# Halving the columns of the score levels, feeding output tiles by k-tile, dividing the query product and adding unread products in a two-block fp32 kernel

## The reference

```python
# block 1: one mixer of two halves, then a pool mixer, a conv FFN behind each
z = h @ w_in                                   # q, f, i, g of HGRN; q, k, v of window attention
diff = b[:, :, :, None, :] - b[:, :, None, :, :]          # b = cumsum(log f) in a chunk
att = einsum('bhtk,bhsk,bhtsk->bhts', qb, kb, exp(where(causal, diff, -inf)))
o = o_inter + att @ vb                         # 4 heads of 128; S carried from chunk to chunk
y = concat([oa, ob]) @ w_out                   # out1
# block 2, layer 0: Fourier mixing and a gated linear attention in both directions
o_f = gla_scan(q, k, v, loga[0]); o_b = gla_scan(flip(q), flip(k), flip(v), flip(loga[1]))
y = concat([fourier_mix(u_f), norm(o_f + flip(o_b)) * silu(r)]) @ w_out       # out2
# block 2, layer 1: grouped attention, 8 query heads on 2 key heads, 512 queries, 768 keys
q = rope(rms_norm(h @ w_q)); p = softmax(q @ k.T / sqrt(128)); y = (p @ v) @ w_att_out  # attout
# layer norms (block 1) and rms norms (block 2) stand between all stages
```

## Time and profile before

| | |
|---|---|
| median of three executions | 3099.12 us (3098.80 to 3101.23) |
| profiled execution | 3098.91 us |
| its span, first to last instruction | 3097.3 us |
| busy PE / weight loads / DVE / ACT / POOL | 2644.9 (85%) / 2172.8 (70%) / 1810.3 (58%) / 1082.0 (35%) / 21.5 (1%) |
| mean granted TensorE clock | 0.916 |
| DMA | 295.50 MB, mean 95 GB/s |

### The profile page before, as it was taken

One profiled execution on the slowest core, in us unless ns is written; L12 is line 12 of the kernel. 1 busy time (PEld: TensorE's weight loads), 2 busy tenths in 40 slices (PEclk: granted clock), 3 DMA queues, 4 the chain that ended last, 5 costly groups with the idle time before them and its releaser, 6 DMA issues.

```text
span 3097.3 us, 31671 instructions
## 1 busy us (share of the span) xinstructions
PE 2644.9 (85%) x12904; PEld 2172.8 (70%) x12904; DVE 1810.3 (58%) x2446; ACT 1082.0 (35%) x1419; POOL 21.5 (1%) x31
## 2 busy tenths in 40 slices
PE   5945579999659999898655889999998977889998
PEld 4844458888438888687355678888887765768886
DVE  6575568888778877610386255524543556465464
ACT  2242253233353244422222243312332544353242
POOL 0000000000010000000000000000000000000000
PEclk9977789999879999999765799999999998999999
DMA  8700027855115666221000012211121100123232
GB/s 309 237 20 2 31 78 265 275 188 183 47 63 184 198 203 199 67 99 40 18 1 1 21 48 68 68 64 57 66 68 63 41 21 14 54 77 109 87 101 83
DMA packets 80272, 295.50 MB, mean 95 GB/s; under 512 B 8944, under 2 KB 11632, under 8 KB 79872
## 3 DMA queue, kind: packets, MB, share of 16 engines
q1 hardware_dynamic: 80128, 293.49, 28.4%
HBM read 291.35 MB, written 2.10 MB: 95 GB/s over the span
## 4 chain that ended last, share of the span: by engine, by line
PE 77%; DVE 14%; ACT 6%; issue 2%; DMA 0%; POOL 0%; DVEq 0%; ACTq 0%
PE ps L308 65%; PE ps L331 2%; PE ps L2114 1%; PE ps L1668 1%; DVE gatt L672 1%; PE ps L661 1%; DVE p_lo L2384 1%; DVE anm L2366 1%; DVE h_lo L513 1%; DVE w_lo L288 1%; DVE hatt L672 1%; DVE x L1244 0%; DVE x L1257 0%; ACT h_hi L507 0%; PE ps L916 0%
## 5 line engine op out<-in xcount | busy, mean ns | idle before, releaser
L308 PE MATMUL ps<-h_hi,w_hi 128*128 128x512 f32 (+1 forms) x2448 | 821.1, 371 | 90.1 <-DVE w_lo L288 39.2
L308 PE MATMUL ps<-h_lo,w_hi 128*128 128x512 f32 (+1 forms) x2448 | 816.1, 369 | 0.0
L308 PE MATMUL ps<-h_hi,w_lo 128*128 128x512 f32 (+1 forms) x2448 | 815.0, 369 | 0.0
L288 DVE TENSOR_TENSOR w_lo<-w_raw,w_hi 128x1024 fp32r<-128x1024 f32 (+2 forms) x323 | 414.7, 1284 | 573.4 <-ACT w_hi L280 572.5
L280 ACT ACTIVATE w_hi<-w_raw 128x1024 fp32r<-128x1024 f32 (+2 forms) x323 | 357.2, 1106 | 892.9 <-PE ps L308 871.9
L308 PEld LDWEIGHTS ps<-h_hi,w_hi 128*128 128x128 f32 x2448 | 464.3, 190 | 178.7 <-issue 54.8
L308 PEld LDWEIGHTS ps<-h_lo,w_hi 128*128 128x128 f32 x2448 | 464.6, 190 | 78.8 <-issue 1.0
L308 PEld LDWEIGHTS ps<-h_hi,w_lo 128*128 128x128 f32 x2448 | 464.2, 190 | 79.0
L308 PE MATMUL ps<-g_hi,w_hi 128*128 128x512 f32 (+1 forms) x880 | 295.9, 369 | 0.8 <-DVE w_lo L288 0.8
L308 PE MATMUL ps<-g_lo,w_hi 128*128 128x512 f32 (+1 forms) x880 | 294.9, 368 | 0.0
L308 PE MATMUL ps<-g_hi,w_lo 128*128 128x512 f32 (+1 forms) x880 | 294.9, 368 | 0.0
(11 more groups left out here) (370 smaller groups left out, 2724.7 us busy)
## 6 DMA issues: line engine op xcount, KB each, us to landing
w_raw<-in_up SPq DMA_DIRECT2D x176, 512.0 KB, 3.3
m_raw<-in_w_mod SPq DMA_DIRECT2D x96, 512.0 KB, 3.3
w_raw<-in_down SPq DMA_DIRECT2D x64, 704.0 KB, 4.1
m_raw<-in_ada_w SPq DMA_DIRECT2D x83, 512.0 KB, 4.7
w_raw<-in_in SPq DMA_DIRECT2D x39, 512.0 KB, 3.3
w_raw<-in_out SPq DMA_DIRECT2D x16, 512.0 KB, 3.3
m_start<-in_ada_w SPq DMA_DIRECT2D x13, 512.0 KB, 12.0
w_raw<-in_qkv SPq DMA_DIRECT2D x12, 512.0 KB, 3.2
```

The source lines that it names most:

```text
L288: dve.tensor_tensor(k.w_lo[s][:, 0:w], k.w_raw[s][:, 0:w], k.w_hi[s][:, 0:w].bitcast(F32), ALU.subtract).then_inc(*k.tick("w_lo", g))
L308: last = pe.matmul(ps[:, bank, 0:tn], a[:, c, :], b[:, c, t0:t0 + tn], start=c == 0 and n == 0, stop=c == kt - 1 and n == 2)
```

## The change

Four parts.

1. **Half-column levels.** Step 0 and levels 0 and 1 stay whole. From level 2 on PE multiplies only the receiving half of each unit's columns (64, taken with strides from the same operand), the results lie side by side, and DVE's copy takes half as many columns. Such a step has two groups (HGRN 8 and 8 units, GLA 8 and 16) and its banks alternate by the step's parity: 4 to 7 and 0 to 3. The masks are 1664 columns (HGRN) and 5760 (GLA) where they were 1024 and 1920; SP loads 704 and 1280. POOL makes them with one cast per step, repeating them, 8 and 15 casts where there was one each.
2. **Output tiles.** out1: ACT splits tile 1 ahead of the vectors. out2: tiles 0 and 1 as a pair, each k-tile as soon as it is there; tile 1's split goes into GLA's loop of the heads. attout: tiles 0 and 1 in parts inside the last period and around mix 7, and tile 1's split ahead of mix 7's copy.
3. **Divided query product.** Chunks 0 to 2 at t=0, 3 and 4 at t=1, 5 to 7 at t=3, each part ahead of the score; in bank 3, the sum, rotation and mixes in bank 1, mix 7 in bank 0. ACT's copy of the product stands at t=3, what follows it (sum, root, norm, rotation, q_hi, q_lo) a period later, at t=0, 1 and 3. Head 0 to 5's h_hi and h_lo move from periods 7 to 9 to periods 8 and 9.
4. **Fillers.** pe_sums puts 8 products of ones by ones (128 columns, float32) ahead of its wait and 14 behind the sums; nobody reads them.

```diff
+def is_wide(steps, i):
+    return i == 0 or steps[i - 1][1] < WIDE
+def halves(a, step):
+    backward, level = step
+    half = 1 << level
+    return a.rearrange("p (n c) -> p n c", c=2 * half)[:, :, 0 if backward else half:half if backward else 2 * half]
...
+def pool_masks(k, label, masks, att, directions):
+    pool, src, at = k.nc.gpsimd, mask_stage(att, directions), 0
+    steps = (HG_STEPS, GL_STEPS)[directions - 1]
+    for i in range(len(steps) + 1):
+        n = mask_width(steps, i)
+        part = src[:, at:at + n]
+        last = pool.tensor_copy(mask_of(masks, steps, i).rearrange("p (u c) -> p u c", c=n), part.unsqueeze(1).to_broadcast([P, 1 if n == P else 4 * directions, n]))
+        at += n
+    last.then_inc(*k.tick("masks", label))
...
+def score_groups(steps, i, n_units):
+    if is_wide(steps, i):
+        return [(0, 4, 4), (8, 12, 4)] if n_units == 16 else [(0, 4, 4), (8, 16, 4), (12, 20, 4)]
+    return [(0, 4, 4), (8, 12, 4)] if n_units == 16 else [(0, 4, 4), (8, 16, 8)]
+def score_bank(steps, i, g):
+    return 4 + 2 * (g % 2) if is_wide(steps, i) else (4 if i % 2 else 0) + 2 * g
+def pe_scores(k, label, i, lhs, rhs, units, steps):
+    pe, wide, groups = k.nc.tensor, is_wide(steps, i), score_groups(steps, i, len(units))
+    before = max([j for j in range(i) if (wide or i % 2 if is_wide(steps, j) else j % 2 == (1 if wide else i % 2))], default=None)
+    for g, (first, second, n) in enumerate(groups):
+        if wide and g >= 2:
+            pe.wait_ge(*k.seen("att", (label, i, g - 2)))
+        elif before is not None and is_wide(steps, before) and wide:
+            pe.wait_ge(*k.seen("att", (label, before, g if g + 2 >= len(groups) else g + 2)))
+        elif before is not None:
+            pe.wait_ge(*k.seen("att", (label, before, len(score_groups(steps, before, len(units))) - 1 if wide or is_wide(steps, before) else g)))
+        bank = score_bank(steps, i, g)
+        for u in range(n):
+            for side, at in enumerate((first, second)):
+                rows, cols = units[at + u]
+                width = mask_width(steps, i)
+                out, right = k.ps[:, bank + side, u * width:(u + 1) * width], rhs[rows, cols]
+                if not wide:
+                    out, right = out.rearrange("p (n c) -> p n c", c=1 << steps[i - 1][1]), halves(right, steps[i - 1])
+                last = pe.matmul(out, lhs[rows, cols], right, start=True, stop=True)
+        last.then_inc(*k.tick("scored", (label, i, g)))
+def dve_scores(k, label, i, att, masks, n_units, steps):
+    dve, mask = k.nc.vector, mask_of(masks, steps, i)
+    if i:
+        dve.wait_ge(*k.seen("att", (label, i - 1, len(score_groups(steps, i - 1, n_units)) - 1)))
+    for g, (first, second, n) in enumerate(score_groups(steps, i, n_units)):
+        dve.wait_ge(*k.seen("scored", (label, i, g)))
+        bank = score_bank(steps, i, g)
+        got = k.ps[:, bank:bank + 2, :]
+        dst = att[:, first:second + n, :].rearrange("p u c -> p (u c)")
+        if second - first > n:
+            dst = att[:, 8:24, :].rearrange("p (s u) c -> p s u c", s=2)[:, :, first - 8:first - 8 + n, :].rearrange("p s u c -> p s (u c)")
+        else:
+            dst = dst.rearrange("p (s c) -> p s c", s=2)
+        if is_wide(steps, i):
+            dst, got = (a.rearrange("p s (u c) -> p s u c", c=P) for a in (dst, got))
+            chosen = mask.unsqueeze(1).unsqueeze(1).to_broadcast([P, 2, 4, P])
+        else:
+            backward, level = steps[i - 1]
+            half = 1 << level
+            dst = dst.rearrange("p s (n c) -> p s n c", c=2 * half)[:, :, :, 0 if backward else half:half if backward else 2 * half]
+            got = got[:, :, 0:n * P // 2].rearrange("p s (n c) -> p s n c", c=half)
+            chosen = mask[:, 0:n * P // 2].rearrange("p (n c) -> p n c", c=half).unsqueeze(1).to_broadcast([P, 2, n * P // 2 // half, half])
+        dve.copy_predicated(dst, chosen, got).then_inc(*k.tick("att", (label, i, g)))
...
+def pe_filler(k, n):
+    for _ in range(n):
+        k.nc.tensor.matmul(k.ps[:, 4, 0:P], k.ones[:, :], k.ones[:, :], start=True, stop=True)
...
+    pe_filler(k, 8)
...
+    pe_filler(k, 14)
...
+        if h == 3:
+            act_split(k, BASE["out2"] + 1)
...
+    ready = [("h_lo", ("fourier", c)) for c in range(4)] + [("h_lo", ("gla", c)) for c in range(4, KD)]
+    pe_residual(k, BASE["out2"], TALL, k.h_hi, k.h_lo, ready, ("rms", 1), paired=True)
...
+PARTS = [range(0, 3), range(3, 5), range(0), range(5, 8)]
+QUERY_BANK, SUM_BANK = 3, 1
...
     for p in range(2, PERIODS):
-        if p < HEADS:
-            pe_query(k, p, [("roped", ("q", p - 1 if p > 2 else 0, "sin"))])
-        if p == 2:
-            pe_query_turn(k, 1)
         for t, s in enumerate(steps_of(p)):
+            if p < HEADS:
+                pe_query(k, p, PARTS[t])
+            if p == PERIODS - 1:
+                pe_attout_part(k, 0, (range(2), range(2, 3), range(3, 4), range(4, 5))[t])
             pe_score(k, s)
             if t == 2 and p >= 3:
                 pe_mix(k, p - 3)
             if s >= 2:
                 pe_probs(k, s - 2)
-            if t == 1 and p < HEADS:
-                pe_query_sum(k, p)
-            if t == 2 and p < HEADS:
-                pe_query_turn(k, p)
-    for s in (4 * HEADS - 2, 4 * HEADS - 1):
-        pe_probs(k, s)
+            if t == 0 and p <= HEADS:
+                pe_query_sum(k, p - 1)
+            if t == 1 and p <= HEADS:
+                pe_query_turn(k, p - 1)
+    pe_probs(k, 4 * HEADS - 2)
+    pe_attout_part(k, 0, range(5, 6))
+    pe_probs(k, 4 * HEADS - 1)
+    pe_attout_part(k, 1, range(2))
     pe_mix(k, HEADS - 1)
-def pe_query(k, p, free):
-    pe_product(k, QKV + 4 + p, LAT, k.h_hi, k.h_lo, (), at_bank(p), free)
+    pe_attout_part(k, 1, range(2, 6))
+    for c in (6, 7):
+        for n in range(2):
+            pe_attout_part(k, n, range(c, c + 1))
...
+def mix_bank(h):
+    return SUM_BANK if h < HEADS - 1 else 0
...
+            if t == 0 and p == 2:
+                act_query(k, 1)
+            if t == 0 and p < HEADS:
+                act_split(k, QKV + 4 + p + 1)
+            if t == 3 and p < HEADS:
+                act_query(k, p)
+            if t == 1 and p <= HEADS:
+                act_query_root(k, p - 1)
             act_at_exp(k, s)
             if t == 2 and p >= 3:
                 act_mixed(k, p - 3)
             if s >= 2:
                 act_probs(k, s - 2)
-            if t == 1 and p < HEADS:
-                act_query_root(k, p)
-            if t == 3 and p < HEADS:
-                act_query_high(k, p)
-            if p >= HEADS - 1:
-                act_head_high(k, {(7, 0): 0, (7, 1): 1, (7, 2): 2, (7, 3): 3, (8, 0): 4, (9, 0): 5}.get((p, t)))
+            if t == 3 and p <= HEADS:
+                act_query_high(k, p - 1)
+            for h in HIGH_PARTS.get((p, t), ()):
+                act_head_high(k, h)
     for s in (4 * HEADS - 2, 4 * HEADS - 1):
         act_probs(k, s)
     act_head_high(k, HEADS - 2)
+    act_split(k, BASE["attout"] + 1)
     act_mixed(k, HEADS - 1)
     act_head_high(k, HEADS - 1)
+HIGH_PARTS = {(8, 0): (0,), (8, 1): (1,), (8, 2): (2,), (8, 3): (3,), (9, 0): (4,), (9, 1): (5,)}
+LOW_PARTS = {(8, 1): (0,), (8, 2): (1,), (8, 3): (2,), (9, 0): (3,), (9, 1): (4,), (9, 2): (5,)}
...
+            if t == 0 and p < HEADS:
+                dve_split(k, QKV + 4 + p + 1)
             dve_at_max(k, s)
+            if t == 1 and p <= HEADS:
+                dve_query_normed(k, p - 1)
             if s:
                 dve_at_probs(k, s - 1)
-            if t == 2 and p < HEADS:
-                dve_query_normed(k, p)
             if s >= 2:
                 dve_probs_low(k, s - 2)
-            if t == 3 and p < HEADS:
-                dve_rope(k, ("q", p), k.q_raw[p % 2], at_bank(p), ("q", p - 1))
-                dve_query_low(k, p)
-            if p >= HEADS - 1:
-                dve_head_low(k, {(7, 1): 0, (7, 2): 1, (7, 3): 2, (8, 0): 3, (8, 1): 4, (9, 1): 5}.get((p, t)))
+            if t == 1 and p <= HEADS:
+                dve_rope(k, ("q", p - 1), k.q_raw[(p - 1) % 2], SUM_BANK, ("q", p - 2))
+            if t == 3 and p <= HEADS:
+                dve_query_low(k, p - 1)
+            for h in LOW_PARTS.get((p, t), ()):
+                dve_head_low(k, h)
     dve_at_probs(k, 4 * HEADS - 1)
     for s in (4 * HEADS - 2, 4 * HEADS - 1):
         dve_probs_low(k, s)
     dve_head_low(k, HEADS - 2)
+    dve_split(k, BASE["attout"] + 1)
     dve_head_low(k, HEADS - 1)
...
     act_window(k)
+    act_split(k, BASE["out1"] + 1)
     act_vectors(k)
     act_tables(k)
-    act_residual(k, BASE["out1"], ("ln", 0), BASE["up", 0, 0, 0] + 1)
+    act_residual(k, BASE["out1"], ("ln", 0), BASE["up", 0, 0, 0] + 1, ahead=1)
```

More of the change, by code:

```diff
@@ L34 @@
 LATS = slice(CTX, TALL)
+WIDE = 2
 WINDOW = 16
@@ L647 @@
 INTERLEAVED = [0, 4, 1, 5, 2, 6, 3, 7]
-def pe_scores(k, label, i, lhs, rhs, units):
-    pe = k.nc.tensor
-    for b in range(0, len(units), 8):
```

(19 more changed lines are left out.)

181 lines of the change are left out of this document (95 added, 86 removed).

## The result

The change makes the kernel faster: 3047.89 us median of four executions (3045.56 to 3054.54) against 3099.32; the ratio is 0.9836 with a 95% interval of 0.9819 to 0.9853. That is -51 us where -72 was forecast (3028), inside the stated range. Run again beside the experiments the changed kernel has 3047.02 (3044.39 to 3053.34).

What follows compares the result with a forecast made beforehand. It took GLA's levels as bound by DVE and the attention as a serial chain through three engines, none full. Terms: -6 - 18 + 0.5 - 9 - 6 - 28.5 - 5 = -72, giving 3028 us; range 3003 to 3058.

Steps and rivals of the forecast that it cites:

- HGRN, -6 forecast: HGRN's half-column levels: halved copies on DVE save 1.08 us per narrow level; -6 us in all (-4 to -8).
- Four of them save 4.3: HGRN's five narrow scored steps: four save 4.3 us together; the last, where DVE waits for PE, gives 1.7 (0 to 3.8).
- GLA, -18 forecast: GLA's half-column levels: smaller copies and a removed DVE wait shorten narrow steps to 5.3 us; -18 us (-12 to -24).
- the 5.7 drawn from the load rule: GLA's narrow loop: if loads cost by 128 weight columns whatever the moving width, some 5.7 us, not 5.3; GLA -15.
- The attention, -28.5 forecast: Attention with divided query product: period 25.5 to 21.6 us, five periods -19.5, first -11; with attout -28.5 (-14 to -37).
- That goes to about 2462: Attention's first maximum, at 2467.64, comes at about 2462, as product 2 and rotation 1 no longer stand ahead.
- t=2 5.0: Attention period's step t=2 takes 5.0 us, since mix waits for the rope's sine and starts earlier.
- out1: First output product: with the split put ahead, tile 1 runs warm and tile 2 starts earlier; -9 us (-8 to -9.5).
- out2: Output product after GLA: chunks of tiles 0 and 1 fill PE's idle 6.02 us before the last h_lo; -6 (-4 to -7).
- Fillers, -5 forecast: Eight sums, each with 22 unread products: if the clock holds, 0.7 to 1.7 us saved in half; -5 (-8 to +4).
- Rival 1: Narrow levels give little: PE's loads hold the step, or copies stay slow; HGRN -2, GLA -4, 3046 us; chance 0.15.
- Rival 3: Slower: PE at half clock throughout the attention because the product lies in pieces between waits; 3112 us; chance 0.03.

Runs made afterwards that it cites:

- e2: Changed kernel, but in HGRN's narrow steps PE multiplies all 128 columns of a unit and DVE copies only the receiving half: 3038.74 us.
- e7: Changed kernel, HGRN still narrow, with two unread products of 256 columns on PE behind each group of eight: 3034.68 us, one execution.
- e9: Changed kernel with HGRN products whole, copies half, q_hi and q_lo a step earlier, weight split later; added: ACT's query 1 copy before k_hi and q_hi: 3038.04 us.
- e4: Changed kernel with all eight chunks of the query product in one piece at the head of step 0: 3054.22 us.
- e6: Changed kernel with the output-tile part undone in out1, out2 and attout (splits and product order of the kernel before): 3062.46 us.
- e3: Changed kernel without the unread products around the eight sums: 3046.23 us.

## Why the prediction came out as it did

- **HGRN, -6 forecast, +5.9 measured: the step that failed.** "Four of them save 4.3; in the last, DVE waits for PE ... it gives 1.7". The bound was worked out from DVE's rows alone; PE's were not read for this stretch, where the kernel before alternates between 3.81 and 5.44 us a step at a granted clock of 0.89, and where a step at half clock (7.0 us) is longer than the 5.8 that DVE would need. Loads set PE's pace; halving the columns left the time per record and took away the work by which the clock was granted. e2 and e7 show it from both sides. Being busy did not keep the clock up: PE was busy 29.2 of 30 us at 0.50. I weighed the load rule for GLA and not here, where loads follow each other half as fast.
- **GLA, -18 forecast, -24.4 measured**, at the good end of its range: loop 5.20, and the half clock cost nothing since loads and DVE are level (the 5.7 drawn from the load rule was too long: 48 loads at the 0.110 of rows 6 are 5.3). But 2.7 of the 24.4 lie ahead of step 3, where nothing is narrow; with the same instructions this stretch takes 37.5 to 40.3 us in the traces, 40.3 in the kernel before. From step 3 on the gain is 20.7 to 21.6 in all ten traces without fill in GLA, and that is the change's. It is made of 12.6 in the five forward steps (forecast 10 to 12.2), 7.8 in steps 10 to 12 (6 to 7.4) and 1.2 in the last two (1.3 to 6.8), where DVE now waits 4.4 for PE. The wide steps 8 and 9 got no new wait in this trace, but one of 1.00 in six of those ten, as I had feared.
- **The masks** (+0.5) cost nothing here: POOL's 15 casts took 11.99 us, 4.7 more than the slope gave, and its clearing ended at 1529.94, 2.4 ahead of the first copy.
- **The attention, -28.5 forecast, -20.9 measured**, by two terms of 3.5 us each. "That goes to about 2462": measured from the FFN's sum the first maximum gained 2.1, not 5.6. I overlooked that with one bank for all query products the first part waits for the copy of query 1, which the change also moved behind key 1's and query 0's high parts on ACT (4.61 idle, then 4.0 cold); e9 moves it back and gains 4.4. The five periods gained 16.1 where 19.5 was forecast. "t=2 5.0": the mix's 4.2 us on PE stay whole on the path, 7.09, while step 1 took 5.45 for 6.2. The sum 21.6 against 22.13 was near by luck. Why it is shorter I had half wrong: e4 shows that it is not the division.
- **out1** (-9.2) came as worked out: PE waits 0.27 for tile 2's w_lo and starts it 12.3 us after tile 0 where it was 21.3; undone in e6, 8.0 of it are gone. **out2** had the size, with an uncertainty from the clock that I did not state. **attout** gained nothing that the traces can tell, as forecast.
- **Fillers, -5 forecast**: at most 1 to 2 (e3). They can act only where the sum runs at half clock, which was so in four of eight sums before and, with the rest of the change, in two of eight without fillers; in one of these two they helped. (Rows 12 do not show the 0.45 that I took for a record at full clock; two of 512 columns take 1.12 together.)
- Rival 1 (loads pace the step) was the right mechanism in the wrong stage: I gave it 0.15, argued it from GLA's rows and priced HGRN at -2 by it, where +5.9 came. Rival 3, half clock throughout, was written for the attention and did not come there (0.98 granted in its five periods, 0.96 before); HGRN is where it happened. Its reason fell too: whole, the product has 0.94 granted (e4), in parts 0.98.
- That the total lay inside the range is partly luck: HGRN missed by 12 us and the attention by 8 in one direction, GLA by 3 to 6 in the other, and the range was wide enough for the rest.

What stays open: why an execution has its FFN at 228 or 233 records in 40 us; why the clock of GLA's heads falls in some executions; how much of the shorter period is the late chain and how much the bank.

## What to carry to other kernels

Before work is taken off an engine's stream, read two rows: the rate of its loads, which narrower operands don't change, and the granted clock on which it stands; if the loads bound it, fewer columns per load give nothing and can cost the clock. Take the saving where the bound is: here the half copies on DVE, with the products left whole. And where a product waits for a copy, ask which bank makes it wait and where the copy stands in its own engine's list: a shared bank and a copy moved back cost PE an idle of 4.6 us here.
